# Three edits in a mixer layer's middle: a reciprocal made by ScalarE's exponential, a value's transposes ahead of a fill, a weighing ahead of a fill

## The reference

```
proj = x @ w_in                                    # columns shared out among the branches
a = silu(layer_norm(conv31(a_u * sigmoid(a_v)))) * silu(a_gate)   @ p_a
b = (b_b * conv3(b_c * b_h)) * silu(b_gate)                        @ p_b
logf = log_sigmoid(c_f + b_forget); cum = cumsum(logf)             # 8 heads
c = softmax(q k^T / 8 + cum[t] - cum[s], causal) v * silu(c_gate)  @ p_c    # 8 heads of 64
m = softmax(m_q mk^T / 8) mv * silu(m_gate)                        @ p_m    # 4 heads, 256 memory tokens
x = layer_norm(alpha * x + (sum of sigmoid(g_i) * branch_i) @ w_out)
```

## Time and profile before

| | |
|---|---|
| median of 3 runs | 1236.19 us |
| the profiled execution | 1234.27 us |
| its span, first to last instruction | 1232.5 us |
| outside the span | 1.8 us |
| mean granted TensorE clock | 0.998 |
| busy: PE / DVE / ACT / POOL | 98% / 62% / 44% / 62% |
| TensorE idle in the list of waits, all | 22.5 us, of which 6.0 at the very start |

### The profile page before, as it was taken

One profiled execution on the slowest core, in us unless ns is written; L12 is line 12 of the kernel. 1 busy time (PEld: TensorE's weight loads), 2 busy tenths in 40 slices (PEclk: granted clock), 3 DMA queues, 4 the chain that ended last, 5 costly groups with the idle time before them and its releaser, 6 DMA issues.

```text
span 1232.5 us, 15758 instructions
## 1 busy us (share of the span) xinstructions
PE 1202.4 (98%) x5704; PEld 998.8 (81%) x5704; DVE 767.5 (62%) x1254; ACT 538.6 (44%) x991; POOL 758.7 (62%) x582
## 2 busy tenths in 40 slices
PE   8999999999999999999999999999999999999997
PEld 6888888888888888888878878878788788878886
DVE  5623865676665755347695564565655776876755
ACT  5433424344434444566344655646555443415000
POOL 6677787877876877877128666677664225557000
PEclk9999999999999999999999999999999999999999
DMA  8012131132332332335222011112002433377141
GB/s 275 9 60 69 35 103 55 66 120 104 102 137 103 103 117 89 137 105 187 87 66 55 24 46 52 35 52 52 18 18 86 165 134 112 111 244 248 63 137 69
DMA packets 91277, 118.61 MB, mean 96 GB/s; under 512 B 6072, under 2 KB 72632, under 8 KB 91200
## 3 DMA queue, kind: packets, MB, share of 16 engines
q1 hardware_dynamic: 91200, 117.60, 29.2%
HBM read 92.39 MB, written 25.20 MB: 95 GB/s over the span
## 4 chain that ended last, share of the span: by engine, by line
PE 84%; DVE 8%; POOL 3%; ACT 2%; issue 2%; DMA 1%; DVEq 0%; SPq 0%; ACTq 0%; POOLq 0%
PE pj L744 11%; PE pj L745 11%; PE pj L746 11%; PE pj L816 4%; PE pj L815 4%; PE pj L817 4%; PE pj L1074 4%; PE pt L745 3%; PE pt L746 3%; PE pt L744 3%; PE po L929 3%; PE pt L916 3%; PE pj L832 2%; PE pj L833 2%; PE pj L834 2%
## 5 line engine op out<-in xcount | busy, mean ns | idle before, releaser
L1569 POOL TENSOR_TENSOR ring_lo<-w_pair,ring_hi 128x512 fp32r<-128x512 f32 x168 | 232.5, 1386 | 110.7 <-ACT ring_hi L1130 110.5
L1622 POOL TENSOR_TENSOR w_lo<-w_raw,w_hi 128x128 fp32r<-128x128 f32 (+1 forms) x104 | 105.1, 1031 | 126.5 <-ACT w_hi L1220 124.4
L1659 POOL TENSOR_SCALAR probs<-probs,rinv 128x128 f32<-128x128 f32 (+3 forms) x64 | 126.4, 1975 | 90.8 <-DVE rinv L2099 90.6
L1130 ACT ACTIVATE ring_hi<-w_pair 128x512 fp32r<-128x512 f32 x168 | 105.1, 628 | 160.6 <-PE pj L746 108.6
L1780 DVE SCALAR_TENSOR_TENSOR po<-glu,cwa,po 128x512 f32<-128x512 f32 x232 | 159.4, 747 | 20.6 <-ACT po L1181 20.6
L744 PE MATMUL pj<-t_hi,ring_hi 128*128 128x512 f32 x392 | 152.8, 390 | 0.3 <-DVE slot L1744 0.3
L745 PE MATMUL pj<-t_lo,ring_hi 128*128 128x512 f32 x392 | 152.5, 389 | 0.0
L746 PE MATMUL pj<-t_hi,ring_lo 128*128 128x512 f32 x392 | 152.5, 389 | 0.0
L815 PE MATMUL pj<-xT_hi,w_hi 128*128 128x512 f32 x320 | 126.0, 394 | 0.0
L816 PE MATMUL pj<-xT_lo,w_hi 128*128 128x512 f32 x320 | 125.5, 392 | 0.0
L817 PE MATMUL pj<-xT_hi,w_lo 128*128 128x512 f32 x320 | 125.1, 391 | 0.0
(11 more groups left out here) (343 smaller groups left out, 2939.1 us busy)
## 6 DMA issues: line engine op xcount, KB each, us to landing
w_pair<-in_w_in SPq DMA_DIRECT2D x28, 1024.0 KB, 5.3
gate_scratch<-slot SPq DMA_DIRECT2D x16, 1024.0 KB, 4.0
gate<-gate_scratch SPq DMA_DIRECT2D x32, 512.0 KB, 3.8
w_raw<-in_w_in SPq DMA_DIRECT2D x20, 512.0 KB, 3.9
z_scratch<-slot SPq DMA_DIRECT2D x8, 512.0 KB, 2.6
bias<-cum_scratch SPq DMA_DIRECT2D x8, 512.0 KB, 4.2
wout_raw<-in_w_out SPq DMA_DIRECT2D x8, 512.0 KB, 5.7
x_tok<-in_x SPq DMA_DIRECT2D x8, 512.0 KB, 4.4
```

Source lines behind the costliest of these rows:

```text
L1130: nc.scalar.activation(ring_hi[:, j % RING, :, :], w_src(u, p), ACT.Copy).then_inc(s_rhi, 1)
L1569: nc.gpsimd.tensor_tensor(ring_lo[:, j % RING, :, :], w_src(u, p), ring_hi[:, j % RING, :, :], ALU.subtract).then_inc(s_rlo, 1)
L1622: nc.gpsimd.tensor_tensor(w_lo[:, j % 2, k, :], w_raw[:, j % 2, k, :], w_hi[:, j % 2, k, :], ALU.subtract).then_inc(s_wlo, 1)
L1659: nc.gpsimd.tensor_scalar(probs[:, u % 2, 0:(i + 1) * P], probs[:, u % 2, 0:(i + 1) * P], rinv[:, u % 2, 0:1], None, ALU.mult).then_inc(s_ ...
```

## The change

First, `f_r` is made by ScalarE as `exp(-ln(f_u))` right behind the logarithm, ahead of tile 2's weight split; VectorE's reciprocal goes, and its product waits for ScalarE's result instead. The counts of `s_fv` are one lower. Second, in unit 1 of each pair `turn_v(c)` is issued ahead of the unit's fill, and 3 k-steps of fill instead of 2 stand before `turn(c, 1)` (1 instead of 2 behind it). Third, the last `weigh` of the last pair is issued right behind the memory's first two scores, ahead of the first 5 k-steps of `m_fill`.

```
-        F_STEPS = 9
+        F_STEPS = 8
...
-                    cut = 4 * u + (3 if u == 0 else 2)
+                    cut = 4 * u + (3 if u < 2 else 2)
+                    if u == 1:
+                        turn_v(c)
                     stream_part(s + S_C, S_C, 4 * u, cut)
                     if u == 0 and c:
                         weigh(c - 1, UNITS // 2 - 1)
-                    if u == 1:
-                        turn_v(c)
                     turn(c, u)
...
             mscores(0)
             mscores(1)
+            weigh(CT - 1, UNITS // 2 - 1)
             for w in range(2 * NT):
                 m_fill(PER * w, PER * w + 5)
-                if w == 0:
-                    weigh(CT - 1, UNITS // 2 - 1)
                 pe.wait_ge(s_pn, UN + w + 1)
...
             nc.scalar.activation(f_l[:, :], f_u[:, :], ACT.Ln).then_inc(s_fa, 1)
+            act.wait_ge(s_fa, 6)
+            nc.scalar.activation(f_r[:, :], f_l[:, :], ACT.Exp, scale=-1.0).then_inc(s_fa, 1)
             split_w(1, 0)
...
-            nc.vector.reciprocal(f_r[:, :], f_u[:, :]).then_inc(s_fv, 1)
-            dve.wait_ge(s_fv, 4)
+            dve.wait_ge(s_fv, 3)
+            dve.wait_ge(s_fa, 7)
             nc.vector.scalar_tensor_tensor(out=f_e[:, :], in0=f_e[:, :], scalar=-1.0, in1=f_r[:, :],
                                            op0=ALU.mult, op1=ALU.mult).then_inc(s_fv, 1)
-            dve.wait_ge(s_fa, 6)
```

More of the change, by code:

```diff
@@ L2023, in _ @@
                                            op0=ALU.subtract, op1=ALU.subtract).then_inc(s_fv, 1)
-            nc.vector.reciprocal(f_r[:, :], f_u[:, :]).then_inc(s_fv, 1)
-            dve.wait_ge(s_fv, 4)
+            dve.wait_ge(s_fv, 3)
+            dve.wait_ge(s_fa, 7)
             nc.vector.scalar_tensor_tensor(out=f_e[:, :], in0=f_e[:, :], scalar=-1.0, in1=f_r[:, :],
                                            op0=ALU.mult, op1=ALU.mult).then_inc(s_fv, 1)
-            dve.wait_ge(s_fa, 6)
-            dve.wait_ge(s_fv, 5)
+            dve.wait_ge(s_fv, 4)
             nc.vector.tensor_tensor(f_l[:, :], f_l[:, :], f_e[:, :], ALU.add).then_inc(s_fv, 1)
             nc.vector.tensor_scalar(f_z[:, :], f_z[:, :], -1.0, 0.0, ALU.mult, ALU.max).then_inc(s_fv, 1)
-            dve.wait_ge(s_fv, 7)
+            dve.wait_ge(s_fv, 6)
             nc.vector.tensor_tensor(f_l[:, :], f_l[:, :], f_z[:, :], ALU.add).then_inc(s_fv, 1)
             dve.wait_ge(s_fone, 1)
-            dve.wait_ge(s_fv, 8)
+            dve.wait_ge(s_fv, 7)
             nc.vector.tensor_tensor_scan(negcum[:, :], f_one[:, :], f_l[:, :], 0.0, ALU.mult,
```

## The result

The changed kernel takes 1227.04 us (median of 6 runs, 1226.17 to 1227.98), the kernel before 1236.21 in the same comparison (6 runs, 1234.76 to 1237.3). The ratio is 0.9927, with a 95% interval of 0.9914 to 0.9939: 9.0 us faster, between 7.5 and 10.6. The profiled execution took 1226.17 with a span of 1224.4. The forecast was 1230.5 and its range ended at 1228.2, so the direction was right and the gain was forecast too small by 3.3 us. In the comparisons further down 94 more runs of the kernel before have a median of 1235.5 and all 11 runs of the changed one 1227.2, so some 0.7 of the 9.0 us is how the six runs of the kernel before fell here.

A forecast was written before the change was run, and what follows sets the result against it. It took TensorE, busy for 98% of the span, as the bound. Head 1.9 + pairs 1.4 + weighing 2.4 = 5.7 us, so 1236.19 - 5.7 = 1230.5 us; range 1228.2 to 1234.2.

The forecast's parts named there:

- The reading of the bound: Whole kernel: TensorE is busy 98% of the span, so an edit is worth what it takes from TensorE's standing still.
- the head: TensorE's 2.63 us wait for the last `k_stack_lo`: ScalarE's exponential replacing VectorE's reciprocal gains 1.9 us, bounds 1.3 and 2.9.
- the pairs: Value's transposes earlier in unit 1: 0.47 us in each of pairs 1 to 3, nothing in pair 0; 1.4 in sum.
- the weighing: Last weighing right behind the memory's first scores: both `za_lo` stalls go, 2.74 less 0.3 cost, 2.4 us gained.
- The exponential's end: In the head on ScalarE: with a table load of 1.28 charged, it ends at 622.60, 4.27 us earlier than the reciprocal.
- The meeting: In the head: GpSimd's tile 2 weight split now stands beside VectorE's two-input operations and delays VectorE by 2.5 us.
- The second term: In the head: tile 3's split again gets in front of the last `k_stack_lo`, moving its end from 640.3 up to 641.0.
- The stall that was to stay: In the head: 0.4 to 1.1 us of TensorE's wait for `k_stack_lo` would remain.
- Rival (a): Head covered whole, GpSimd's split and VectorE's sums not holding each other up: 2.9 instead of 1.9, time 1229.5; chance 0.20.
- the change of shape: In the pairs: one more change from transposes to full matmuls on TensorE costs 0.1 us.
- the `probs` stalls: In pairs 1 to 3: TensorE's 0.9 us waits for GpSimd stay as long, since that chain moves with the value's low part.
- L2190: In the memory's attention: this little VectorE operation still waits for GpSimd's 2.41 us product to end, 1.76 us, moving along.

The follow-up runs named there:

- head_only: The kernel before with only the exponential in place of the reciprocal: 1232.4 us, ratio 0.9973.
- split_first: The changed kernel with ScalarE's split of tile 2 ahead of the exponential instead of behind it: 1226.98 us, ratio 0.9933 against the kernel before.
- before_again: The kernel before, unedited, timed against itself for a second profile: 1235.45 us, ratio 1.0004.
- weigh_only: The kernel before with only the last weighing moved ahead of the memory's first fill: 1232.24 us, ratio 0.9975.
- stall_filled: The kernel before with 12 unread matmuls of 512 columns in the head's long stall: 1236.81 us, ratio 1.0007.
- both_filled: The kernel before with unread matmuls in both long stalls, 12 in the head, 8 and 2 before the `za_lo` k-steps: 1234.36 us, ratio 0.9989.

## Why the prediction was wrong, point by point

**The reading of the bound** held: TensorE's work is what it was, and the time went with three of its stalls.

**The size of the miss.** The forecast gain of 5.7 us was 3.3 too small. The mechanisms that it named were right; its terms were mis-sized or left out: the head by 0.8, the pairs by 0.7, the weighing by 0.1, the waits for `gate` behind it by 0.6, and the lowered clock behind the stalls, put at nothing, by 0.6 to 1.4.

**The head: forecast 1.9, measured 2.7** (2.71, 2.66 and 2.81 in the traces of after, `head_only` and `split_first`, against the 591.5 of the unchanged head; the last has no meeting). The exponential's end was right to 0.03, table load included. The meeting was real and in the place named, but its price was mis-sized: GpSimd's whole 2.5 us were charged to VectorE, and 2.0 is what it lost. The second term, tile 3's split getting in front of the last `k_stack_lo`, was on the wrong side: in the earlier trace rows VectorE paid 0.43, here it started first and paid nothing. The stall that was to stay, 0.4 to 1.1, is 0.15. Rival (a), 2.9, was nearer, but by luck: its condition, that the two don't hold each other up, didn't hold. The rule of the Trainium skill on the port pair (page "SBUF — State Buffer", section "SBUF: two separate sides") agrees with 1.63 for 1.21 and 4.21 for 2.50. VectorE's dearest row there, 2.29 for 0.67, is an operation with one input, of which the prediction's sentence says nothing. That the rule speaks against the edit wasn't borne out, since the loss fell into spare time.

**The pairs: forecast 3 x 0.47 + 0, measured 2.0 to 2.1**: 0.65, 0.62 and 0.65 in pairs 1 to 3 (the distance of the two traces grows so) and 0.16 in pair 0. Each step of the count is in the rows. From the fill's first matmul the second half went at 1.69 (forecast 1.75) and the turn at 4.27 (forecast 4.30, and 0.1 more for the change of shape). Most of the difference is in these rows. The 0.1 was a little too much: the three k-steps with the change in them take 724.27 - 722.11 = 2.16 instead of 2.08, and the transposes gave 0.03 back. Some of the rest is a stall's tail (what its end costs beyond the idle time) that was left out here: the turn behind the old stall took 0.41, now 0.38. That the `probs` stalls would stay as they were was right (0.95 and 0.91), and so was its reason: with the value's low part GpSimd's `probs` came 0.65 earlier, measured from the fill's first matmul (4.80 and 4.15).

**The weighing: forecast 2.4.** It cost 0.28 by the stage up to `za_hi` (forecast 0.3), both `za_lo` waits went (2.74), and GpSimd's product and L2190 met as foretold (1.76 and 1.74). By these rows it is 2.5, a hit. The stage as a whole gave 0.6 more.

**The sum.** 2.7 + 2.1 + 2.5 = 7.3 by the rows of the named terms, where 5.7 was forecast. With the 0.6 of the stage, 7.9. What the runs gave is 9.0 (7.5 to 10.6) and 8.3 (6.7 to 10.0).

**The step that was missing** is what comes behind a stall. The prediction says that a stall that vanishes gives back its idle time and 0.27 us, and has no term for the clock behind it: it puts that at nothing without a reason. The traces show that a long one can be followed by a spell of half clock: 1.36 and 1.34 us in `before_again` and `weigh_only`, 1.6 in `stall_filled`. Of seven profiles of kernels in which one or both long stalls stood, three have such a spell; of seven of kernels in which they are gone or filled, none. Three in seven times 1.4 us is an estimated 0.6 us in a mean run, 55 in 94 an estimated 0.8, and `both_filled` measures 1.4 (0.2 to 2.3). So the named rows, the stage's rest and the spells together give 8.5 to 9.3, and 9.0 and 8.3 were timed. The forecast was made from a profile that happened to have no spell, and a profile without one can't show it.

**The range** failed with it: its low end was the sum of the bounds, 7.4 us, less 0.6 for the runs' spread. All three terms came out near or above their upper bounds (2.7 of 2.9, 2.1 of 1.8, 2.5 of 2.7), and no bound held the spell.

**Open.** The 0.6 us of the stage behind `za_hi` lies at the waits for `gate` and `merged`, but why isn't explained: these waits vary by as much from trace to trace, and 13 traces don't separate their mean from an effect of the order. Why the spell follows a stall in one execution and not in the next was not found out; of the seven profiles with a long stall the three with a spell are those whose first stage was longest (52.66 to 52.87 us, against 51.09 to 52.33), so it may hang on when the stall falls, and not all of the 1.9 us between the two groups of runs need be the spell's. How much filling the stalls gains rests on one comparison whose interval ends at 0.9998. `both_filled` adds matmuls to both stalls at once; filling the one for `za_lo` alone was not tried, and why `stall_filled` was long even at 0.999 stays open.

## What to carry to other kernels

A stall's price is its idle time and its tail, and, where it is like the long ones here (1.8 to 2.6 us), what the clock may do behind it; read several profiles of the same kernel before calling it nothing. When VectorE and GpSimd meet, work out both outcomes, since the same pair of operations cost both engines in one trace and GpSimd alone in the next, where VectorE had started first, and ask who has time to spare. When a wait shortens and the time stands still, look at the engine behind the next wait for work in its row that nobody needs yet: moving one 2.40 us product by five units gave 3 us, and only then was the finer order of the transposes worth anything.

## What the runs showed of the hardware

- TensorE at 98% of the span fell to its lower level behind one stall of 2.63 us, for about 3.4 us, the last 0.4 of the stall among them (`before_again`): 512 columns 0.43 us apart instead of 0.23, granted clock 0.76 over the 5 us behind it. In another execution of the same kernel it stayed at 1.00. The Trainium skill, page "TensorE: Matmul & The Clock Gate", Part 1, says that the clock is gated by how busy the engine was of late and knows two levels; these pitches are those two levels.
- The table load between a logarithm and an exponential took 1.28 us (changed kernel), and the exponential began 0.02 behind it; the whole switch cost 1.31 us.
- GpSimd and VectorE each lengthened the other in the head by 1.7 us (4.21 for 2.50) and 2.0 us; at the second meeting only GpSimd's operation was longer, by 1.0. In the kernel before that meeting cost GpSimd 1.0 and VectorE 0.43.
